# Operand and weight addresses modulo 64 bytes in a one-layer hybrid encoder step

## What is computed

```python
def _swiglu_half(x, g, w_gate, w_up, w_down):
    h = _rmsnorm(x, g)
    return 0.5 * ((jax.nn.silu(h @ w_gate) * (h @ w_up)) @ w_down)

x = x + _swiglu_half(x, g_ffn1, w1_gate, w1_up, w1_down)
z = _rmsnorm(x, g_mix) @ w_in           # q, k, v | mq, mk, mv, mo, gates
x = x + concat(attention, _rmsnorm(sigmoid(mo) * h_mlstm)) @ w_out
x = x + _swiglu_half(x, g_ffn2, w2_gate, w2_up, w2_down)
y = _rmsnorm(x, g_final)
```

## Time and profile before

| | us |
|---|---|
| median of 3 executions | 1949.27 |
| lowest, highest | 1944.7, 1949.57 |
| the profiled execution | 1950.25 |
| its span, first to last instruction | 1948.7 |
| TensorE busy with matmuls | 1927.9 |
| VectorE, ScalarE, GpSimd busy | 1279.4, 783.2, 1051.0 |
| mean granted TensorE clock | 0.997 |

### The profile page before, as it was taken

One profiled execution on the slowest core, in us unless ns is written; L12 is line 12 of the kernel. 1 busy time (PEld: TensorE's weight loads), 2 busy tenths in 40 slices (PEclk: granted clock), 3 DMA queues, 4 the chain that ended last, 5 costly groups with the idle time before them and its releaser, 6 DMA issues.

```text
span 1948.7 us, 39225 instructions
## 1 busy us (share of the span) xinstructions
PE 1927.9 (99%) x14627; PEld 1885.3 (97%) x14627; DVE 1279.4 (66%) x1882; ACT 783.2 (40%) x1595; POOL 1051.0 (54%) x958
## 2 busy tenths in 40 slices
PE   8999999999999999999999999999999999999998
PEld 7999999999999999999998999999999999999997
DVE  7766776666466778854445664866767667646674
ACT  6433333333443345733334542443333333344343
POOL 2277776775777641321222442237767776676770
PEclk9999999999999999999999999999999999999999
DMA  8135455344986530333332735214454444498552
GB/s 270 45 114 181 135 168 173 132 133 155 317 309 190 168 100 20 116 113 92 97 103 62 208 98 119 78 56 144 147 181 145 132 154 164 152 355 277 167 156 103
DMA packets 226846, 293.88 MB, mean 151 GB/s; under 512 B 16616, under 2 KB 158472, under 8 KB 226736
## 3 DMA queue, kind: packets, MB, share of 16 engines
q1 hardware_dynamic: 219040, 272.76, 43.8%
q0 software_dynamic: 7696, 19.63, 3.2%
HBM read 198.07 MB, written 94.21 MB: 150 GB/s over the span
## 4 chain that ended last, share of the span: by engine, by line
PE 94%; DMA 2%; DVE 2%; issue 1%; ACT 1%; POOL 1%; SPq 0%; ACTq 0%; POOLq 0%
PE bank L292 29%; PE bank L294 29%; PE bank L293 28%; PE bank L2584 1%; PE bank L2603 1%; PE bank L2594 1%; DMA WRAW<-in_w_down 1%; DMA XIN<-in_x_prompt 1%; DMA ZO<-zm 1%; PE bank L2515 0%; PE bank L1333 0%; PE bank L1335 0%; PE bank L1334 0%; PE bank L1329 0%; PE bank L846 0%
## 5 line engine op out<-in xcount | busy, mean ns | idle before, releaser
L292 PE MATMUL bank<-HA,HW 128*128 128x272 f32 x1120 | 322.4, 288 | 0.6 <-DVE HW L1382 0.6
L294 PE MATMUL bank<-HA,HW 128*128 128x272 f32 x1120 | 322.6, 288 | 0.0
L293 PE MATMUL bank<-HA,HW 128*128 128x272 f32 x1120 | 322.0, 287 | 0.0
L1382 DVE SCALAR_TENSOR_TENSOR HW<-WRAW,HW 128x512 fp32r<-128x512 f32 x140 | 221.2, 1617 | 108.7 <-ACT HW L1377 108.4
L1388 POOL TENSOR_TENSOR HA<-ARAW,HA 128x544 fp32r<-128x544 f32 x140 | 220.7, 1591 | 104.9 <-ACT HA L1376 104.5
L292 PE MATMUL bank<-HH,WGH 128*128 128x362 f32 (+2 forms) x784 | 256.4, 327 | 0.0
L294 PE MATMUL bank<-HH,WGL 128*128 128x362 f32 (+2 forms) x784 | 247.0, 315 | 1.9 <-issue 1.9
L293 PE MATMUL bank<-HL,WGH 128*128 128x362 f32 (+2 forms) x784 | 247.0, 315 | 0.0
L294 PE MATMUL bank<-FC,WR 128*128 128x272 f32 x768 | 222.1, 289 | 0.0
L292 PE MATMUL bank<-FC,WR 128*128 128x272 f32 x768 | 220.9, 288 | 0.6 <-DVE WR L584 0.5
L293 PE MATMUL bank<-FC,WR 128*128 128x272 f32 x768 | 219.8, 286 | 0.0
(11 more groups left out here) (384 smaller groups left out, 5667.6 us busy)
## 6 DMA issues: line engine op xcount, KB each, us to landing
asp<-SA SPq DMA_DIRECT2D x44, 544.0 KB, 3.5
RAWG<-in_w_gate SPq DMA_DIRECT2D x22, 1024.0 KB, 6.5
RAWU<-in_w_up SPq DMA_DIRECT2D x22, 1024.0 KB, 6.4
tsp<-TT SPq DMA_DIRECT2D x40, 544.0 KB, 6.5
ARAW<-tsp SPq DMA_DIRECT2D x80, 272.0 KB, 3.4
WS<-in_w_down SPq DMA_DIRECT2D x20, 1024.0 KB, 8.7
wsp<-WS SPq DMA_DIRECT2D x20, 1024.0 KB, 8.5
WRAW<-wsp SPq DMA_DIRECT2D x80, 256.0 KB, 4.4
```

Source lines behind the costliest of these rows:

```text
L292: nc.tensor.matmul(bank[:, 0:w], w_hi, rhs_hi, start=first, stop=False)
L293: nc.tensor.matmul(bank[:, 0:w], w_hi, rhs_lo, start=False, stop=False)
L294: return nc.tensor.matmul(bank[:, 0:w], w_lo, rhs_hi, start=False, stop=last)
L1382: nc.vector.scalar_tensor_tensor(out=HW[f][h][:, 1], in0=WRAW[r][:, :], scalar=0.5, in1=HW[f][h][:, 0].bitcast(F32), op0=ALU.mult, op1=ALU ...
```

## The change

No instruction is added, removed or reordered. Only SBUF addresses change.

- The regions are put in another order (wg first) and 16 bytes are put ahead of HH, HL and A.
- The single tensor `WR` becomes eight, slot o at 0, 8, 16, 24, 32, 40, 48 and 48 bytes more than its multiple of 4096.
- `WGH`, `WGL` stay 24 bytes off a multiple of 64. `SS` moves by 64 bytes.
- The `HA` pieces all start at a multiple of 64; the `HW` pieces stand at 40 (slots 0, 1), 56 (slots 2, 3) and 8 (slots 4, 5) modulo 64.
- Small constants share tiles (three in GQOE, two each in GATES, TOPS, SUMS), which frees the bytes for this.

Worked out from the sizes, the starts modulo 64 are:

| | before | after |
|---|---|---|
| region X (FX of FFN 1, FB of FFN 2, HH) | 0 | 32 |
| region HH (FB of FFN 1, FX of FFN 2) | 0 | 48 |
| region HL (FC, HL) | 0 | 0 |
| region A (FT, AB) | 0 | 16 |
| WR slots 0 to 6 | all 24 | 0, 8, 16, 24, 32, 40, 48 |
| WGH, WGL | 24 | 24 |
| HA, HW, slots 0 to 5 | 0, 24 and 32, 56 in turn | 0, 40; 0, 40; 0, 56; 0, 56; 0, 8; 0, 8 |

The core of the diff:

```diff
-WEIGHTS = 24
+CONSTANTS = 5408
-        rX = region("x", KT * T * 4)
-        rHH = region("hh", KT * T * 4)
-        rHL = region("hl", KT * T * 4)
-        rA = region("a", 4 * T * 4)
-        region("lead", WEIGHTS)
-        rWG = region("wg", 2 * 4 * 4096)
-        region("rest", 32 - WEIGHTS)
+        rWG = region("wg", 2 * 4 * 4096 + 64)
         rRAW = region("raw", 4 * 4096)
         rD = region("d", 3 * 8192)
         rT = region("t", 8 * NW * 4)
-        rC = region("c", 0)
+        rC = region("c", CONSTANTS)
+        rX = region("x", KT * T * 4)
+        region("before_hh", 16)
+        rHH = region("hh", KT * T * 4)
+        region("before_hl", 16)
+        rHL = region("hl", KT * T * 4)
+        region("before_a", 16)
+        rA = region("a", 4 * T * 4)
...
-        WGH = place("WGH", [P, 4, KT, P], F32R, rWG)
-        WGL = place("WGL", [P, 4, KT, P], F32R, rWG + 4 * 4096)
+        WGH = place("WGH", [P, 4, KT, P], F32R, rWG + 24)
+        WGL = place("WGL", [P, 4, KT, P], F32R, rWG + 4 * 4096 + 24)
...
-        WR = place("WR", [P, PRODUCTS + 1, 2, 4, P], F32R, rWG)
-        SS = place("SS", [P, 2, 4, P], F32, rWG + PRODUCTS * 4096)
+        WR = [place(f"WR{o}", [P, 2, 4, P], F32R, rWG + 4096 * o + lead) for o, lead in enumerate((0, 8, 16, 24, 32, 40, 48, 48))]
+        SS = place("SS", [P, 2, 4, P], F32, rWG + PRODUCTS * 4096 + 64)
...
-        slot_at = [[rHL, rHL + 8480, rHL + 17408, rHL + 17408 + 8480, o_ + 17408, o_ + 26112] for o_ in (rX, rHH)]
-        HA = [[place(f"HA{f}{h}", [P, 2, 2, HT], F32R, slot_at[f][h]) for h in range(SLOTS)] for f in range(2)]
-        HW = [[place(f"HW{f}{h}", [P, 2, 512], F32R, slot_at[f][h] + 4352 + WEIGHTS) for h in range(SLOTS)] for f in range(2)]
+        slot_at = [[rHL, rHL + 8576, rHL + 17408, rHL + 17408 + 8576, o_ + 17408, o_ + 26112] for o_ in (rX, rHH)]
+        places = ((0, 40), (0, 56), (0, 8))
+        HA = [[place(f"HA{f}{h}", [P, 2, 2, HT], F32R, (slot_at[f][h] + 63) // 64 * 64 + places[h // 2][0]) for h in range(SLOTS)] for f in range(2)]
+        HW = [[place(f"HW{f}{h}", [P, 2, 512], F32R, (slot_at[f][h] + 63) // 64 * 64 + 4352 + places[h // 2][1]) for h in range(SLOTS)] for f in range(2)]
...
-        GQ = small("GQ", [2])
-        GO = small("GO", [LH])
+        gains = small("GQOE", [2 + LH + 1])
+        GQ, GO, EPSC = gains[:, 0:2], gains[:, 2:2 + LH], gains[:, 2 + LH:3 + LH]
...
-                    mm = three_pass(BANK[o], HT, WR[:, o, 0, k], WR[:, o, 1, k], product(o, j, 0, k, f), product(o, j, 1, k, f), k == 0, k == 3)
+                    mm = three_pass(BANK[o], HT, WR[o][:, 0, k], WR[o][:, 1, k], product(o, j, 0, k, f), product(o, j, 1, k, f), k == 0, k == 3)
```

More of the change, by code:

```diff
@@ L96, in build @@
         rT = region("t", 8 * NW * 4)
-        rC = region("c", 0)
-        assert base + rC < nc.sbuf_usable_end
+        rC = region("c", CONSTANTS)
[6 more added lines that the diff above has]
+        rA = region("a", 4 * T * 4)
+        assert base + at["end"] <= nc.sbuf_usable_end
         X = place("X", [P, KT, T], F32, rX)
@@ L209, in build @@
         GC = small("GC", [3, KT])
-        GQ = small("GQ", [2])
-        GO = small("GO", [LH])
+        gains = small("GQOE", [2 + LH + 1])
+        GQ, GO, EPSC = gains[:, 0:2], gains[:, 2:2 + LH], gains[:, 2 + LH:3 + LH]
         SINK = small("SINK", [HEADS])
         NSINK = small("NSINK", [HEADS])
[L214 to L220, removed]
+        gates = small("GATES", [5])
+        GATE, GBF = gates[0:LH, 0:4], gates[0:32 + LH, 4:5]
+        tops = small("TOPS", [8])
+        NMX, SUM = tops[:, 0:4], tops[:, 4:8]
+        sums = small("SUMS", [8])
+        ESK, DEN = sums[:, 0:4], sums[:, 4:8]
         FS = small("FS", [4, 4])
@@ L225, in build @@
         RMB = small("RMB", [NB + 1, LH])
-        assert base + small_at <= nc.sbuf_usable_end
+        assert small_at <= rC + CONSTANTS
         BANK = [ctx.enter_context(nc.psum_tensor(f"bank{i}", [P, 512], F32)) for i in range(8)]
@@ L578, in weight_high @@
                 act.wait_ge(s_.mm, p * 28 + (280 * f - 28 + 14 * mat - 7 + o + 1))
-            nc.scalar.activation(WR[:, o, 0], weight(o, q0, mat), ACT.Copy).then_inc(s_.hi, 1)
+            nc.scalar.activation(WR[o][:, 0], weight(o, q0, mat), ACT.Copy).then_inc(s_.hi, 1)
         def weight_low(dve, f, p, mat, o, first=False):
@@ L583, in weight_low @@
             dve.wait_ge(s_.hi, p * 14 + (140 * f - 14 + 7 * mat + o + 1))
-            nc.vector.tensor_tensor(WR[:, o, 1], weight(o, q0, mat), WR[:, o, 0].bitcast(F32), ALU.subtract).then_inc(s_.lo, 1)
+            nc.vector.tensor_tensor(WR[o][:, 1], weight(o, q0, mat), WR[o][:, 0].bitcast(F32), ALU.subtract).then_inc(s_.lo, 1)
         def counts(f, p, mat, j, per):
@@ L961, in start_weight_high @@
                 act.wait_ge(z.mm, C1 + 48 + OUT_STEPS - 4 + i % 4 + 1)
-            nc.scalar.activation(WR[:, i, 0], first_weight(i), ACT.Copy).then_inc(st.whi, 1)
+            nc.scalar.activation(WR[i][:, 0], first_weight(i), ACT.Copy).then_inc(st.whi, 1)
         def start_weight_low(dve, f, i):
             dve.wait_ge(st.whi, 8 * f + i + 1)
-            nc.vector.tensor_tensor(WR[:, i, 1], first_weight(i), WR[:, i, 0].bitcast(F32), ALU.subtract).then_inc(st.wlo, 1)
+            nc.vector.tensor_tensor(WR[i][:, 1], first_weight(i), WR[i][:, 0].bitcast(F32), ALU.subtract).then_inc(st.wlo, 1)
         def start_chain(pe, f, mat, j, i, between=None):
@@ L987, in start_chain @@
                 for k in range(4):
-                    mm = three_pass(BANK[i], HT, WR[:, slot, 0, k], WR[:, slot, 1, k], product(PLACE[e], j, 0, k, f), product(PLACE[e], j, 1, k, f),
+                    mm = three_pass(BANK[i], HT, WR[slot][:, 0, k], WR[slot][:, 1, k], product(PLACE[e], j, 0, k, f), product(PLACE[e], j, 1, k, f),
                                     kh == 0 and k == 0, kh == 1 and k == 3)
```

## The result

The changed kernel takes 1954.04 us (median of 7, 1953.6 to 1955.65), the kernel before 1945.35 us beside it (median of 7, 1944.7 to 1949.57). The ratio is 1.004 with a 95% interval of 1.0028 to 1.0052: slower by 8.7 us, which is over the 0.3% that the prediction set as the bound. The profiled execution of after took 1954.55 us, near its median. That of before, at 1950.25 us, is longer than all seven of those runs, so the two traces differ by only 4.3 us. Compared stage by stage they nevertheless say where the loss is.

A forecast was written before the change was run, and what follows sets the result against it. The prediction took TensorE's matmul count by pitch as the bound. Gate/up 8.6 us and down 8.4 us gained, the rest 0, summed to 17.0 us: 1950.25 - 17.0 = 1933.3 us, range 1910 to 1966 us.

The forecast's parts named there:

- the 0.3%: Whole kernel: a measurement tells some 0.3%, 5.8 us, from no change.
- slower, by the walk from product to product: Gate/up rival: operand and weight starts changing every 12 matmuls cost pitch, 1960.7 to 1982.5 us; chance 0.28.
- The bound: Whole kernel: TensorE bounds it, so time is the number of matmuls by their pitch.
- Length part and place part: Matmul pitch excess: 6.9 ns at 272 columns goes with length; the rest with distance: 5.7 at 0, 0 at 16.
- Unmeasured distances at the mean of the known: Gate/up and down: distances 32, 48, 56 and 8, without rows, taken at 3.2 ns, the mean of four known.
- Down, 8.4 us gained: Down stage, 3360 matmuls: place part falls from 5.7 to 3.2 ns, 2.5 each, 8.4 us gained.
- the jumps: Down stage before: operand start jumps between 0 and 32 every three matmuls; their end is part of the 8.4 us.
- Projections and constants at 0: About 2350 projection matmuls, unmeasured distances, taken as 0 between -11 and +7 us; shared constants add no instruction, 0.
- The thin place at 520 to 530 us: DMAs at 0.99, GpSimd 9.73 of 10 us: TensorE may wait out its gain there; a few us hang on it.
- The walk: Same rival: +10.5 us at 5.7 ns for gate/up alone, 32.2 us at 7.7 for gate/up and down; chance 0.28.
- Its point of decision: Gate/up: the slower rival decides from a mean place part above 4.3 ns.
- Nothing moves: Whole-kernel rival: pitch follows from something else that addresses only seem to explain, 1950 us; chance 0.17.

The follow-up runs named there:

- the uniform run: Changed kernel with all operands at 0, weights of FFN 1 and projections at 16, of FFN 2 at 48 modulo 64: 1960.43 us (single run).
- walk_24: Changed kernel with FFN 1 weights at 24, 8, 56, 8, 40, 24, 56, so every gate/up product there has distance 24: 1953.39 us (single run).
- wr24: Changed kernel with operand regions at 0 and all gate/up weights at 24, down pieces as changed: 1948.41 us (median of 11), 1.0001 of the kernel before.
- wr24_wg8: As wr24, with the projections' weights at 8 in place of 24: 1948.40 us, ratio 1.0004 to the kernel before.
- low_a: Changed kernel, operands 0, high weights 24; low gate/up weights moved 8 (FFN 1), 16 (FFN 2), low down operands and weights 16, 32: 1952.72 us.

## Why the prediction was wrong

The forecast was 1933.3 us and faster; the kernel is slower, at 1954.04 us. That this lies inside the range of 1910 to 1966 is no merit of the mechanism: the range was made wide enough for the rival "slower, by the walk from product to product", which had the sign.

- **The bound** was right: the time is count by pitch, and the idle time next to these stages changed by 1 us. The granted clock was 1.00 in every window.
- **Length part and place part** failed, and this is the step that turned the sign. The values per distance came from stretches of 12 to 24 matmuls at 362 and 364 columns and from other tensors; their length part was scaled to 272 columns, their place part taken over as it was. Measured at 272, distance 16 costs 126.6 ns where the table gave 113.3 + 6.9 + 0 = 120.2, and 24 costs 124.5, where the kernel stood already. That 24 fitted at both lengths (4.3 and 3.7) was taken as confirmation, and was one point. The prediction's own rows had distance 40 twice, at 166.7 and 163.3 ns; it set the first aside because its operand is no multiple of 16. So even at 362 columns the distance doesn't fix the pitch. In the in projection of the kernel with weights at 8, token tile 1 (operand at 48, distance 24) and tile 2 (operand at 24, distance 48) show it; first and last of 18 matmuls each:

```profile
851.85 0.33 PE L296 MATMUL bank<-HH,WGH 128*128 128x362 f32 x1
...
854.85 0.33 PE L296 MATMUL bank<-HH,WGH 128*128 128x362 f32 x1
855.85 0.32 PE L296 MATMUL bank<-HH,WGH 128*128 128x362 f32 x1
...
858.73 0.32 PE L296 MATMUL bank<-HH,WGH 128*128 128x362 f32 x1
```

  3.00 / 18 = 166.7 ns at distance 24, where the earlier trace rows have 164.6; and 2.88 / 18 = 160.0 ns at distance 48, a pitch that the prediction had found at 16 alone. At the start of the in projection, over the eight starts of these weights, distance 24 gave 165.0, 166.7 and 163.5 ns on token tiles 0, 1 and 2, and distance 16 gave 166.6, 164.5 and 166.7.
- **Unmeasured distances at the mean of the known**: a fair rule with a wrong table. With the measured table, the distances of the change give (125.6 + 124.5 + 125.5 + 125.6 + 126.6 + 125.6 + 126.6) / 7 = 125.7 ns in FFN 1 and 125.7 in FFN 2. Measured: 125.47 and 125.63. So the same sum with measured entries would have forecast 1.2 x 7488 = 9 us slower, against 8.2 found. That is in part luck, since only the means agree. Of the two products at distance 16 in FFN 1, product 4 ran at 125.3 ns (median of 40 stages) and product 6 at 126.3, and the uniform run at 126.6. By the prediction's own sign both were to be faster than product 0: product 4 was (125.3 against 125.8), product 6 wasn't. Against before, the seven products lost from 0.5 to 1.8 ns, so the loss isn't the same for all.
- **Down, 8.4 us gained**: 1.2 us were. The excess of 12.6 ns had been read from a window with waits in it, and the jumps, taken to cost 1.4 ns a matmul, cost none.
- **Projections and constants at 0**: held, as far as a stretch can tell that varies by 4 us. The thin place at 520 to 530 us still shows DMAs at 1.02 and GpSimd at 10.00 of 10 us, but TensorE waits only 0.18 us in it (9.82 of 10 us busy), and 0.3 us before the whole group of down products, against 0.6 before.
- **The walk** was priced at 10.5 to 32.2 us; it and the distances together cost 8.2 in gate/up. In walk_24 it cost 0.55 ns at the best distance, 2.1 us for one FFN by pitch and 2.8 by the stage's time. How much of the loss is walk and how much distance stays open: the products that run at two pitches with equal starts fit neither by itself. Its point of decision, a mean place part over 4.3 ns, was reached: 125.5 is 5.3 over 120.2.
- **"Nothing moves"**, which the Trainium skill (TensorE: Matmul & The Clock Gate, Step-by-step: what each phase is for) would give with its two independent read ports, is contradicted: the same instructions ran at 124.5 to 126.6 ns in the windows by addresses alone. Whether the two reads hinder each other is a cause that no run here shows. The estimate of the same page for an isolated matmul (Back-to-back issue gap), 115.8 ns at 272 columns, lies below all of them.

Two things stay open. The first is why these remainders. What is argued and not shown is a rhythm between two streams of reads, that of the moving operand and that of the next weights. For it speaks that the steady pitches are not arbitrary. At distance 16 three matmuls take 0.38 us, in 87% of the groups of three in FFN 1:

```profile
305.83 0.29 PE L298 MATMUL bank<-FXa,WR 128*128 128x272 f32 x1
...
306.21 0.29 PE L298 MATMUL bank<-FXa,WR 128*128 128x272 f32 x1
...
306.59 0.29 PE L298 MATMUL bank<-FXa,WR 128*128 128x272 f32 x1
```

With the trace's times in whole ns the three take 380; at distance 32 they take 373 or 374 in 93% of the groups, in the kernel before in 48%. Both are near whole multiples of 6.667 ns, as are the 160.0 and 166.7 of the projections, and 6.667 ns is 16 columns at 2.4 GHz and one column a cycle, that is 64 bytes of the moving operand. After the change no such repeat stands out (373 or 374 in 22% of the groups), and the pitch lies near the mean over all distances.

The second is what else the pitch hangs on besides the remainders modulo 64, since the two halves of the tokens can differ by 3.3 ns. Their operands lie 128 bytes apart modulo 256, so a longer remainder could be it; the difference between wr24 and wr24_wg8 speaks for a state carried from one stage to the next. No run moved an operand by 64 or 128 bytes alone.

## What to carry to other kernels

Where a long run of matmuls has weights loaded beside it, the pitch can depend on the start addresses of its operands, by up to 1.7% in the mean here. It belongs to the whole repeated sequence (columns, starts, order of the passes and what ran before), so a price per distance is not to be had from it. Measure each candidate uniformly, in hundreds of matmuls at the kernel's own width, look at the pitch of each repeated part and not only at the mean, and keep the best one. Spreading starts over the remainders gave about the mean of what they cost here, and lost against a start that was already among the best. A table read from a few dozen matmuls at another width is no price list, even where one entry agrees.

## What the runs showed of the hardware that wasn't expected

- With all starts equal modulo 64, the two halves of the tokens ran at 124.4 and 126.7 ns (weights at 8), and at 123.3 and 126.7 ns (low_a, FFN 2), stage after stage.
- Moving the weights by 4 bytes (24 to 28) changed the pitch of 272-column fp32r matmuls from 124.5 to 125.9 ns, and by 8 bytes (24 to 32) not at all.
- Over eight uniform remainders the pitch ranges over 2.1 ns, 1.7%. The gate/up stage of FFN 1 takes 471.9 us at 24 (wr24) and 478.7 at 16.
- At 362 columns the range is wider: 18 matmuls in a row ran at 160.0 ns (weights at 8, token tile 2) and at 168.9 ns (weights at 40, token tile 1), over 5%.
- VectorE's busy time in a 200 us window of gate/up rose from 136.6 to 142.6 us with the addresses, at one instruction more (199 and 200), and in the kernel whose time came back it was 140.9. Its cause wasn't looked for.
